# Modulation weights on partition halves: sixteen steps of 256 columns in place of eight of 512, two products a piece in place of four

## What is computed

```python
c_act = jax.nn.silu(c)                    # c: (1, 1024)
mod = c_act @ ada_w[l] + ada_b[l]         # ada_w[l]: (1024, 9216)
sh1, sc1, g1, sh2, sc2, g2, sh3, sc3, g3 = jnp.split(mod, 9, axis=-1)
h = modulate(x, norm_g[l, 0], sh1, sc1)
x = x + 0.5 * g1[:, None] * swiglu(h, ff_w13[l, 0], ff_w2[l, 0])
```

## Time and profile before

| | |
|---|---|
| median of 3 runs | 1523.01 us (1517.4 to 1527.09) |
| the profiled execution | 1518.52 us |
| its span, first to last instruction | 1516.7 us |
| PE busy | 1456.2 us, 96% |
| DVE busy | 1053.7 us, 69% |
| ACT busy | 729.2 us, 48% |
| DMA | 314.21 MB, mean 207 GB/s |
| mean granted clock of PE | 0.99 |

### The profile page before, as it was taken

One profiled execution on the slowest core, in us unless ns is written; L12 is line 12 of the kernel. 1 busy time (PEld: TensorE's weight loads), 2 busy tenths in 40 slices (PEclk: granted clock), 3 DMA queues, 4 the chain that ended last, 5 costly groups with the idle time before them and its releaser, 6 DMA issues.

```text
span 1516.7 us, 18742 instructions
## 1 busy us (share of the span) xinstructions
PE 1456.2 (96%) x7206; PEld 1197.3 (79%) x7206; DVE 1053.7 (69%) x1432; ACT 729.2 (48%) x1101; POOL 75.9 (5%) x133
## 2 busy tenths in 40 slices
PE   8997999999999999998999999899999989999998
PEld 7885777888877888887778888688887867788886
DVE  4897565877777777666477767777777678775544
ACT  6545545444454434364464333544435765554342
POOL 7200000000000000010000000000000000000000
PEclk9999999999999999999999999999999999999999
DMA  8870434687856888634368888588883710566560
GB/s 299 281 249 29 167 111 167 232 302 270 272 189 220 302 271 273 225 123 161 105 234 290 280 264 274 171 281 270 284 280 121 243 46 1 180 193 202 188 208 28
DMA packets 189087, 314.21 MB, mean 207 GB/s; under 512 B 6896, under 2 KB 100440, under 8 KB 189000
## 3 DMA queue, kind: packets, MB, share of 16 engines
q1 hardware_dynamic: 148800, 232.87, 46.9%
q10 hardware_dynamic: 38408, 75.65, 13.7%
q0 software_dynamic: 1792, 4.51, 1.0%
HBM read 311.92 MB, written 1.07 MB: 206 GB/s over the span
## 4 chain that ended last, share of the span: by engine, by line
PE 82%; DVE 9%; ACT 5%; issue 3%; DMA 1%; POOL 1%; ACTq 0%; POOLq 0%; DVEq 0%
PE ps L1162 24%; PE ps L1164 24%; PE ps L1163 23%; PE ps L1171 5%; PE ps L1491 2%; PE ps L1309 2%; DVE wlo L1118 1%; PE ps L1437 1%; DVE rmax L2295 1%; ACT sp L1832 1%; DVE tmp L1986 1%; ACT whi L1101 1%; DVE xn L1933 1%; DVE x L1941 0%; DVE wide L1118 0%
## 5 line engine op out<-in xcount | busy, mean ns | idle before, releaser
L1118 DVE TENSOR_TENSOR wlo<-raw,whi 128x2048 fp32r<-128x2048 f32 (+2 forms) x168 | 381.4, 2273 | 153.1 <-ACT whi L1101 153.0
L1162 PE MATMUL ps<-whi,aT 128*128 128x512 f32 (+3 forms) x1000 | 400.5, 401 | 10.6 <-DVE aTl L1974 6.1
L1164 PE MATMUL ps<-wlo,aT 128*128 128x512 f32 (+3 forms) x1000 | 388.9, 389 | 0.0
L1163 PE MATMUL ps<-whi,aTl 128*128 128x512 f32 (+3 forms) x1000 | 387.7, 388 | 0.0
L1101 ACT ACTIVATE whi<-raw 128x2048 fp32r<-128x2048 f32 (+2 forms) x169 | 319.5, 1895 | 82.7 <-DVE prow L2181 35.9
L1162 PEld LDWEIGHTS ps<-whi,aT 128*128 128x128 f32 x1000 | 188.6, 189 | 54.1 <-issue 11.3
L1164 PEld LDWEIGHTS ps<-wlo,aT 128*128 128x128 f32 x1000 | 188.5, 188 | 39.8
L1163 PEld LDWEIGHTS ps<-whi,aTl 128*128 128x128 f32 x1000 | 189.2, 189 | 34.3
L1778 ACT ACTIVATE hT<-ps 128x256 fp32r<-128x256 f32 (+1 forms) x102 | 42.2, 414 | 340.6 <-PE ps L1171 172.4
L1162 PE MATMUL ps<-whi,hT 128*128 128x512 f32 (+1 forms) x364 | 141.1, 390 | 1.4 <-ACT z L1756 1.4
L1164 PE MATMUL ps<-wlo,hT 128*128 128x512 f32 (+1 forms) x364 | 138.4, 382 | 0.0
(11 more groups left out here) (271 smaller groups left out, 2030.3 us busy)
## 6 DMA issues: line engine op xcount, KB each, us to landing
raw<-in_ff_w SPq DMA_DIRECT2D x176, 512.0 KB, 4.8
raw<-in_ff_w SPq DMA_DIRECT2D x44, 1024.0 KB, 5.1
qT<-in_ada_w ACTq DMA_DIRECT2D x36, 1024.0 KB, 6.7
pT<-in_ada_w ACTq DMA_DIRECT2D x36, 1024.0 KB, 7.2
raw<-in_w_up SPq DMA_DIRECT2D x16, 1024.0 KB, 5.8
raw<-in_w_down SPq DMA_DIRECT2D x16, 1024.0 KB, 5.1
raw<-in_w_in SPq DMA_DIRECT2D x9, 1024.0 KB, 9.8
raw<-in_w_ckv SPq DMA_DIRECT2D x8, 1024.0 KB, 5.5
```

What stands on the lines that cost most here:

```text
L1118: dve.tensor_tensor(lo_of(u), raw_of(u), hi_of(u).bitcast(F32), ALU.subtract).then_inc(w_lo, 1)
L1162: pe.matmul(out_ap, hi, w, start=start, stop=False)
L1163: pe.matmul(out_ap, lo, w, start=False, stop=False)
L1164: return pe.matmul(out_ap, hi, wl, start=False, stop=stop)
```

## The change

A piece still has 512 columns, but its two halves of 256 columns lie on two halves of the partitions. The 1024 rows are cut into sixteen chunks of 64 (`AK`), and partitions 0 to 63 hold columns 0 to 255 of the piece and partitions 64 to 127 columns 256 to 511. So a step of DVE covers 64 rows and all 512 columns as 128 x 256: sixteen steps in place of eight, four of them at each age from 2 to 5. `cact` has sixteen columns, silu(c) in chunks of 64, twice, once on each half of the partitions. The sum `asum` is 128 x 256, and PE needs two products, each with two result columns: the moving operand `halves` (128 x 2) has ones on partitions 0 to 63 in column 0 and on 64 to 127 in column 1. They are one turn, at age 7; the turn at age 8 is gone. DVE adds the bias to four columns at once.

The load of half a piece is now two DMAs of 512 KB, each to 64 partitions, in rows of 1 KB (before: one of 1 MB to 128 partitions in rows of 2 KB); `araw[h]` is an array of 128 x 8 x 256 over the same bytes. In the prologue the row of c is loaded by two DMAs in place of one, `ones` (128 x 128) is gone, and four small memsets for `halves` stand on POOL behind its DMAs.

```diff
-            return [("ada_q", dict(m, q0=2 * (m["age"] - 2), prev=self.ada_t))]
-        if 7 <= m["age"] <= 8:
-            return self.ada_out(m, m["age"] - 7)
+            return [("ada_q", dict(m, q0=4 * (m["age"] - 2), prev=self.ada_t))]
+        if m["age"] == 7:
+            return self.ada_out(m)
...
             def ada_out(m):
...
+                if m["n"] == 0:
+                    pe.wait_ge(halves_set, 4)
                 pe.wait_ge(ada_sum, m["n"] + 1)
                 wait_free(pe, T, lambda j: t)
                 for c in range(2):
-                    k = 2 * m["half"] + c
-                    last = pe.matmul(tbank(t)[:, c:c + 1], asum[:, k * P:(k + 1) * P], ones[:, 0:1],
+                    last = pe.matmul(tbank(t)[:, 2 * c:2 * c + 2], asum[:, c * P:(c + 1) * P], halves[:, :],
                                      start=True, stop=True)
...
-            rows(pr, C_COL, 8, A["c_2"][0].rearrange("(a b) -> a b", b=P))
+            for h in range(2):
+                rows(pr[:, 64 * h:64 * h + 64], C_COL, AK, A["c_2"][0].rearrange("(a b) -> a b", b=64))
...
-                    act.wait_ge(ada_mid, (KC - 1) * (m["n"] - 1) + 5)
-                h, c0 = m["h"], m["b"] * ADA_W
-                wv = A["ada_w_2"][m["layer"]].rearrange("(k p) n -> p k n", p=P)
-                act.dma_start(araw[h], wv[:, 4 * h:4 * h + 4, c0:c0 + ADA_W]).then_inc(ada_loaded[h], 16)
+                    act.wait_ge(ada_mid, (AK - 1) * (m["n"] - 1) + KC + 1)
+                h = m["h"]
+                wv = A["ada_w_2"][m["layer"]].rearrange("(k p) n -> p k n", p=64)
+                for i in range(2):
+                    c0 = m["b"] * ADA_W + i * (ADA_W // 2)
+                    act.dma_start(araw[h][64 * i:64 * i + 64], wv[:, KC * h:KC * h + KC, c0:c0 + ADA_W // 2]).then_inc(ada_loaded[h], 16)
...
-                for q in range(m["q0"], m["q0"] + 2):
+                for q in range(m["q0"], m["q0"] + 4):
...
-                c = 4 * m["b"] + 2 * m["half"]
-                dve.tensor_tensor(mod[:, m["layer"], c:c + 2], tbank(m["t"])[:, 0:2],
-                                  prm2[:, c + 72 * m["layer"]:c + 72 * m["layer"] + 2], ALU.add).then_inc(t_dve, 1)
+                c, c2 = 4 * m["b"], 4 * m["b"] + 72 * m["layer"]
+                dve.tensor_tensor(mod[:, m["layer"], c:c + 4].rearrange("p (h c) -> p c h", c=2),
+                                  tbank(m["t"])[:, 0:4].rearrange("p (c h) -> p c h", h=2),
+                                  prm2[:, c2:c2 + 4].rearrange("p (h c) -> p c h", c=2), ALU.add).then_inc(t_dve, 1)
```

More of the change, by code:

```diff
@@ L31 @@
 ADA_N = 9 * D // ADA_W
+AK = 2 * KC
 NEG = -1e30
@@ L43 @@
 NC = (S - 32) // 16 + 1
-G_MIX, G_CROSS, G_MEM, G_MLP, NORM_G, C_COL, Q_NORM, KV_NORM, CONV_W = 0, 8, 16, 24, 32, 80, 88, 90, 91
+G_MIX, G_CROSS, G_MEM, G_MLP, NORM_G, C_COL, Q_NORM, KV_NORM, CONV_W = 0, 8, 16, 24, 32, 80, 96, 98, 99
 G_DIFF = CONV_W + 12
@@ L381, in ada_step, with ada_out @@
         if 2 <= m["age"] <= 5:
-            return [("ada_q", dict(m, q0=2 * (m["age"] - 2), prev=self.ada_t))]
-        if 7 <= m["age"] <= 8:
-            return self.ada_out(m, m["age"] - 7)
+            return [("ada_q", dict(m, q0=4 * (m["age"] - 2), prev=self.ada_t))]
+        if m["age"] == 7:
+            return self.ada_out(m)
         return []
-    def ada_out(self, m, half):
+    def ada_out(self, m):
         t = self.T.add("D")
         self.ada_t = t
[L391 to L395, removed]
+        self.ada_open.remove(m)
+        self.ada_closed += 1
+        self.ada_done[m["layer"], m["b"]] = t
+        return [("ada_out", dict(m, t=t))]
     def ada_flush(self):
@@ L815, in build @@
         msc = sb("msc", [3, 8])
-        cact = sb("cact", [KC])
+        cact = sb("cact", [AK])
+        halves = sb("halves", [2])
         lamb = sb("lamb", [4, HD])
@@ L872, in build @@
         ada_mid = sem("ada_terms")
+        halves_set = sem("halves_set")
         t_ready, t_act, t_dve = sem("t_ready"), sem("t_act"), sem("t_dve")
@@ L1676, in edge @@
                     act.wait_ge(t_dve, 1)
-                    act.activation(cact[:, :], prm[:, C_COL:C_COL + KC], ACT.Silu).then_inc(cact_ready, 1)
+                    act.activation(cact[:, :], prm[:, C_COL:C_COL + AK], ACT.Silu).then_inc(cact_ready, 1)
                     return
@@ L2169, in ada_terms @@
                     dve.wait_ge(cact_ready, 1)
-                for q in range(m["q0"], m["q0"] + 2):
-                    w, c = araw[q // 4][:, q % 4, :], cact[:, q:q + 1]
-                    if q % 4 == 0:
-                        dve.wait_ge(ada_loaded[q // 4], 16 * (n + 1))
+                for q in range(m["q0"], m["q0"] + 4):
+                    w, c = araw[q // KC][:, q % KC, :], cact[:, q:q + 1]
+                    if q % KC == 0:
+                        dve.wait_ge(ada_loaded[q // KC], 32 * (n + 1))
                     if q == 0:
@@ L2176, in ada_terms @@
                     else:
-                        before = araw[(q - 1) // 4][:, (q - 1) % 4, :]
-                        dve.wait_ge(ada_mid, (KC - 1) * n + q)
-                        if q == KC - 1 and m["prev"] is not None:
+                        before = araw[(q - 1) // KC][:, (q - 1) % KC, :]
+                        dve.wait_ge(ada_mid, (AK - 1) * n + q)
+                        if q == AK - 1 and m["prev"] is not None:
                             dve.wait_ge(t_ready, m["prev"] + 1)
-                        ins = dve.scalar_tensor_tensor(asum if q == KC - 1 else w, w, c, before, ALU.mult, ALU.add)
-                    ins.then_inc(ada_sum if q == KC - 1 else ada_mid, 1)
+                        ins = dve.scalar_tensor_tensor(asum if q == AK - 1 else w, w, c, before, ALU.mult, ALU.add)
+                    ins.then_inc(ada_sum if q == AK - 1 else ada_mid, 1)
             def ada_out(m):
                 dve.wait_ge(t_ready, m["t"] + 1)
-                c = 4 * m["b"] + 2 * m["half"]
-                dve.tensor_tensor(mod[:, m["layer"], c:c + 2], tbank(m["t"])[:, 0:2],
-                                  prm2[:, c + 72 * m["layer"]:c + 72 * m["layer"] + 2], ALU.add).then_inc(t_dve, 1)
+                c, c2 = 4 * m["b"], 4 * m["b"] + 72 * m["layer"]
+                dve.tensor_tensor(mod[:, m["layer"], c:c + 4].rearrange("p (h c) -> p c h", c=2),
+                                  tbank(m["t"])[:, 0:4].rearrange("p (c h) -> p c h", h=2),
+                                  prm2[:, c2:c2 + 4].rearrange("p (h c) -> p c h", c=2), ALU.add).then_inc(t_dve, 1)
             def linear(st):
@@ L2585, in _ @@
             pool.dma_start(gbc[:, :], A["g_final"].partition_broadcast(P)).then_inc(gain_loaded, 16)
+            for h in range(2):
+                for i in range(2):
+                    pool.memset(halves[64 * i:64 * i + 64, h:h + 1], float(h == i)).then_inc(halves_set, 1)
+                    pool.wait_ge(halves_set, 2 * h + i + 1)
             def rms(st):
```

8 lines of the change are left out of this document (3 added, 5 removed).

## The result

The changed kernel takes 1570.97 us (median of 4 runs, 1563.61 to 1581.07), the kernel before 1521.32 us (4 runs). The ratio is 1.033, with a 95% interval of 1.030 to 1.037: 50 us slower, where I had forecast 8 us faster. The profiled execution took 1563.61 us with a span of 1561.9 us, 45.2 us more than before. In the changed kernel the large matmuls stand at L1163 to L1165, the transposes at L1172, the products of the modulation at L1311, the steps at L2180 and L2186, the issue of the loads at L1739, `hT` at L1783 and the high parts at L1102.

A forecast was written before the change was run, and what follows sets the result against it. The prediction took PE, busy 96% of the span, as the bound; -12.2 (products), +3.5 (MLP starts) and +0.3 (prologue) made -8.4 us, from a median of 1523.0 to about 1514.5 us, range 1504 to 1530.

The forecast's parts named there:

- PE's term: On PE's list, 34 of the 36 pairs of modulation products removed gain 0.36 us each: -12.2 us.
- DVE's durations: In the modulation's steps on DVE: 483 ns a step, 360 ns the first, busy time about 1115 us.
- their cover: In the steady part DVE and ACT run ahead of PE, so added work there is hidden: no cost.
- Term 2: At the five MLP starts, where DVE's and ACT's lead is gone: +3.5 us, bounds 0 and 27 us.
- The flushes: Two of the removed pairs stand where PE waits for DVE's sum anyway: no gain taken.
- ACT's term: On ACT's queue, one more issue of 0.37 us a load, 27 us more in all, on an engine at 48%.
- the slow loads: Rival: loads to 64 partitions take the DMA engines twice as long in four long MLPs, +24 us, 1539 us; chance 0.11.
- the lead is used up: Rival: at MLP starts DVE and ACT work in turn, half of 27 us is lost, 1525 us; chance 0.17.

The follow-up runs named there:

- e4: The kernel before with its own loads and four products, its eight steps of 512 columns done as sixteen of 256: 1536.73 us, ratio 1.0086.
- e1: The changed kernel with each half piece loaded by one DMA to 128 partitions in 2 KB rows: 1523.69 us, ratio 1.001.
- e13: e3 with the MLPs' loads issued behind the next high part instead of ahead of `hT`: 1515.74 us, ratio 0.9977.
- e16: e4 with the MLPs' loads issued behind the next high part instead of ahead of `hT`: 1526.72 us, ratio 1.0035.
- e5: The kernel before with each half piece loaded by two DMAs to 128 partitions, 2 chunks each, eight steps kept: 1522.19 us, ratio 1.0007.
- e14: The kernel before with its own loads and eight steps, plus two unused activations (0.94 us) on ACT behind each load from the second piece: 1526.80 us, ratio 1.0056.
- e7: e1 plus two unused activations behind each load from the second piece, to hold ACT's queue 1.29 us as in the changed kernel: 1559.85 us, ratio 1.0245.
- e11: The kernel before with the MLPs' loads issued behind the next high part instead of ahead of `hT`: 1516.10 us, ratio 0.9970.
- e8: As e7 with one unused activation behind each load, to hold ACT's queue 0.94 us: 1541.70 us, ratio 1.0121.
- e2: The changed kernel with both loads of each half piece going to all 128 partitions, 1 KB rows: 1543.87 us, ratio 1.0145.
- e6: The kernel before with each half piece loaded by two DMAs to 64 partitions each, 2 KB rows, eight steps: 1548.87 us, ratio 1.0179.
- e10: The changed kernel with its own loads, issued in the MLPs behind the next high part instead of ahead of `hT`: 1534.67 us, ratio 1.0090.
- e15: e2 with the MLPs' loads issued behind the next high part instead of ahead of `hT`: 1517.12 us, ratio 0.9985.
- e3: The changed kernel with each half piece loaded by one DMA to 128 partitions in 1 KB rows: 1522.38 us, ratio 1.0005.

## Why the prediction was wrong

**PE's term held.** Taking two products off each piece was priced at -12.2 us. e4 against e1 gives -13, e13 against e16 -9, and PE's busy time in e1 is 1444.0 us, 12.2 less than before. In the changed kernel it is 1456.3 us again although 72 products (144 records) are gone: the granted clock was 0.982 there and 0.990 before, and PE stops and starts.

**DVE's durations held, their cover did not.** A step took 484 ns (483 forecast), the first 346 (360), and busy time came to 1112 (1115). The step that failed is the sentence "what is added to DVE or ACT costs nothing until it has eaten their lead", together with the 172.4 us of ACT's waits for PE as the measure of that lead. This sum said that there was room, but not where: in `ff01` of the kernel before the `hT` that wait for PE stand at the ages without a load. Behind a load ACT waits for DVE's step already in the earlier trace rows (4.98 us, `<-DVE pT`), 168.2 us in all, and DVE waits for ACT's parts in turn. There the lead was small: 0.53 us more at each load was free (e5), 0.94 cost 8 us (e14), the sixteen steps 4 us (e4 in the MLPs), and with these steps in place each further us of hold cost more than half of itself (36 us for 0.93 us at each of 70 loads, e7). Term 2 put +3.5 us on the starts of the MLPs; the ring is there in all of their length. The prediction's own upper end for it, 27 us at the first six ages only, was still too narrow. It also put nothing on the attention ahead of the first MLP, where the steps cost some 10 us (e16 against e11, e4). The flushes there were given no gain but no loss either; PE's wait at them grew from 1.6 to 7.0 us, 5.4 us.

**ACT's term was mis-sized.** "An issue takes 0.37 us" was read from one load of 128 partitions that stood alone. To 64 partitions an issue takes 0.60 us, and the second right behind it 0.66: 1.29 us a load, 0.92 more and not 0.37. e7 and e8 price it: the first 0.55 us more (an activation of 0.59 us) cost 18 us and the rest of the hold 18 more. Here one edit sufficed to put ACT, at 46% busy, where over half of each us that it is held is lost.

**DMA was a rival, and it was right in kind.** I took 0 and gave the slow loads 0.11, with engine time at twice 5.8 us as the upper end. By the two rows of q10 a piece takes 10.4 us, 1.8 times as much, and the DMA share in the stage is 1.00 where it was 0.79. The Trainium skill, "SBUF — State Buffer", section "Door 1: The DMA port swizzle (why `[64,N]` ≈ `[32,N]`)", gives 196 GB/s for partitions 0 to 63 against 328 for all 128, both at 1 MiB, which is two thirds more time. The runs, with loads of 512 KB, agree with it: 373 us of the engines here against 230 in e2 (14.9% of 1542.3 us), which has the same bytes and rows, is 1.62 times as much, and 22.5% against 13.9% of the span in e6 and e5 is 1.65 times; the rest of the 1.8 is the shorter rows. Its price was 5 to 11 us in the changed kernel, behind the ring, 18 us where the ring was out of the way (e10 against e15) and 19 where it was shorter (e6 against e14); the rival's 24 us is near that. Rows of 1 KB by themselves were priced at 0, and e3 bears that out.

So two rivals came true at once, "the lead is used up", with a ring in all of the MLPs in place of their starts, and "the loads are slow". The sum by the runs, each against the one before it: steps +14, products -13 (e1), the second issue +20 (e2), the longer issues to 64 partitions +16 (e7 against e2), the DMA engines, by what is left, +11.

**PE's clock had no term.** The mean granted clock was 0.975 to 0.982, 0.977 at the median, in the four runs of the changed kernel and 0.982 to 0.994, 0.987 at the median, in 100 runs of the kernel before. Among these 100 runs alone, those at 0.982 took 1526.8 us on average and those at 0.992 took 1517.3, some 0.95 us for each 0.001. By that 9 to 10 of the 50 us go with the clock, an estimate; it is a part of the sums above and not a further one, and no run shows it by itself.

## What to carry to other kernels

Before work is called hidden behind an engine's waits, look at what ends those waits at the very instructions the change touches: an engine at 46% busy can be in a ring with another, and then a good part of each us added to it shows in the time. A DMA issue that has to wait for another engine is placed behind the long operation that others need, not ahead of it. And where a layout fills half of the partitions with one load each, price both the engines' time, 1.6 to 1.8 times as much, and the queue's, 1.3 us in place of 0.4; one load to all partitions, even with half the row, was free.

## What the runs showed of the hardware

- The time an issue holds ACT's queue depends on the partitions written, not on the rows: 374 ns at the least for 256 or 512 rows of 2 KB or 512 or 1024 rows of 1 KB to 128 partitions (e5, before, e2, e3), 602 ns for 256 rows of 2 KB or 512 of 1 KB to 64 (e6, the changed kernel). Two in a row take 0.90 to 0.94 us to 128 partitions and 1.27 to 1.29 us to 64.
- The same bytes to 64 partitions in each load take 22.5 to 23.9% of the DMA engines over the span, to 128 partitions 13.4 to 15.3%, with rows of 1 or 2 KB.
- An issue that waits for nothing runs beside an activation: in e10 two issues began at 846.30 us and took 1.29 us, under a high part from 846.22 to 848.14.
